# Page requests of the sample group's attention: a block's second sequence asked for by ScalarE, its first by SyncE

## The reference

```python
xn = rmsnorm(x, ln1_g)
qa, ka, va, pb, gates = jnp.split(xn @ w_in, SPLIT_IN, axis=-1)
y_a = attend(qa, ka, va).reshape(B, T, WIDTH_A) @ w_br_a          # block-sparse attention
y_b, wkv_new, shift_new = rwkv7_branch(pb, ...); y_b = y_b @ w_br_b  # a recurrence over the tokens
h = x + (g_a * y_a + g_b * y_b) @ w_o
... ConvFFN: w_up, causal convolution, SiLU gate, w_down, final rmsnorm

# attention of the sample group (moba_sample), for each of 8 sequences and 8 heads
k_full = cache_k[page_table]      # 32 pages of 128 tokens = 16 blocks of 256 tokens
gate = q . mean(k of a block);  the best 3 blocks of each query are kept
probs = softmax over the kept blocks and the 8 new tokens;  out = probs @ v
```

## Time and profile before

| what | value |
|---|---|
| median of 3 executions (range) | 1322.64 us (1315.37 to 1325.59) |
| the profiled execution: its own time, its span | 1318.78 us, 1316.7 us |
| mean granted TensorE clock | 0.976 of full speed |
| PE busy over the span | 1212.2 us, 92% |
| ACT busy over the span | 409.8 us, 31% |
| bytes moved by all transfers | 216.28 MB, of which 142.80 MB from 210 to 654 us |

### The profile page before, as it was taken

How to read it: one execution, slowest core, us unless ns; L and a number is a source line. 1 busy time by engine, 2 the same in 40 slices (tenths; PEclk the granted TensorE clock), 3 DMA queues, 4 the chain that set the end, 5 groups by cost and what they waited for, 6 DMA issues and landing times. The chain is left out here.

```text
span 1316.7 us, 33244 instructions
## 1 busy us (share of the span) xinstructions
PE 1212.2 (92%) x14362; PEld 1105.5 (84%) x14362; DVE 628.0 (48%) x1066; ACT 409.8 (31%) x765; POOL 433.4 (33%) x299
## 2 busy tenths in 40 slices
PE   6999997998889888976789999989999999999995
PEld 6988996666766667654589999989999999999994
DVE  6467896444554654555662223234555544470003
ACT  5142331333334332223522222333344333342110
POOL 2333453001110111010123334625555555563440
PEclk9999999999999999998789999999999999999998
DMA  5221215997898789798312222221222222222211
GB/s 210 97 101 72 72 51 232 389 346 292 303 386 329 276 328 380 279 368 304 128 64 82 81 81 97 82 90 65 81 84 92 82 81 81 93 89 89 89 57 72
DMA packets 57252, 216.28 MB, mean 164 GB/s; under 512 B 6610, under 2 KB 6995, under 8 KB 56339
## 3 DMA queue, kind: packets, MB, share of 16 engines
q1 hardware_dynamic: 57106, 214.17, 44.2%
HBM read 207.78 MB, written 6.37 MB: 163 GB/s over the span
## 5 line engine op out<-in xcount | busy, mean ns | idle before, releaser
L642 PE MATMUL ps<-buffer_at 128*128 128x288 f32 (+2 forms) x5760 | 778.3, 298 | 9.9 <-POOL buffer_at L1459 5.0
L642 PEld LDWEIGHTS ps<-buffer_at 128*128 128x128 f32 x5760 | 774.1, 191 | 15.1 <-issue 9.2
L1459 POOL TENSOR_TENSOR buffer_at<-buffer_at 128x1024 fp32r<-128x1024 f32 (+1 forms) x118 | 331.1, 2807 | 359.5 <-ACT buffer_at L1192 358.9
L1192 ACT ACTIVATE buffer_at<-buffer_at 128x1024 fp32r<-128x1024 f32 (+1 forms) x118 | 128.9, 1095 | 288.1 <-PE ps L642 135.0
L1511 POOL TENSOR_TENSOR buffer_at<-buffer_at 128x256 f32<-128x256 f32 x45 | 40.3, 925 | 320.7 <-DVE buffer_at L1751 320.7
L2113 DVE TENSOR_TENSOR buffer_at<-ps,buffer_at 128x512 f32<-128x512 f32 x44 | 30.4, 692 | 126.1 <-PE ps L642 126.1
L1430 ACT ACTIVATE buffer_at<-buffer_at 128x592 f32<-128x592 f32 x44 | 38.8, 882 | 162.4 <-DVE buffer_at L2115 159.2
L1027 PE MATMUL ps<-buffer_at 128*32 128x128 f32 x2048 | 73.5, 282 | 8.4 <-issue 5.2
L1851 DVE TENSOR_REDUCE buffer_at<-ps 128x1 f32<-128x256 f32 (+1 forms) x68 | 28.0, 411 | 109.1 <-PE ps L994 108.9
L994 PE MATMUL ps<-buffer_at 128*32 128x256 f32 x1024 | 69.6, 384 | 5.5 <-DMA buffer_at<-in_kvcache 4.2
L1027 PEld LDWEIGHTS ps<-buffer_at 128*32 128x32 f32 x2048 | 54.4, 112 | 19.3 <-issue 11.5
(11 more groups left out here) (230 smaller groups left out, 1293.9 us busy)
## 6 DMA issues: line engine op xcount, KB each, us to landing
buffer_at<-in_kvcache SPq DMA_DIRECT2D x256, 512.0 KB, 6.1
buffer_at<-in_w_up SPq DMA_DIRECT2D x44, 512.0 KB, 3.5
buffer_at<-in_w_in SPq DMA_DIRECT2D x42, 512.0 KB, 3.5
buffer_at<-in_w_down SPq DMA_DIRECT2D x16, 704.0 KB, 4.1
buffer_at<-in_w_br SPq DMA_DIRECT2D x8, 512.0 KB, 3.5
buffer_at<-in_w_o SPq DMA_DIRECT2D x8, 512.0 KB, 3.5
buffer_at<-in_xin SPq DMA_DIRECT2D x4, 576.0 KB, 7.1
buffer_at<-in_xin SPq DMA_DIRECT2D x1, 2304.0 KB, 11.1
```

The costliest lines, as they stand in the source:

```text
L642: ins = e.matmul(out, lhs, rhs[:, cols], start=(start and i == 0), stop=(stop and i == 2))
L1192: e.activation(hi[:, :, :], raw, ACT.Copy).then_inc(w_hi, 1)
L1459: e.tensor_tensor(lo[:, :, :], raw, hi[:, :, :], ALU.subtract).then_inc(w_lo, 1)
```

## The change

A helper pages_of loads the two page numbers of one sequence into registers of the engine named, and a helper pages_in requests its two pages on that engine. The first three fills stay with SP whole. For each later fill (61 of them) SP loads and requests only the pair's first sequence, after the same wait as before. The second sequence is ACT's: in step i it loads the page numbers of fill step_fill(i) + 3 behind pt_out(i), and requests the two pages behind o_out(i), that is behind the wait for the pv_step whose slot they go into. Each slot still counts four landings.

```diff
+        def pages_of(f, s, engine):
+            at = (2 * (f // NBLK) + s) * NPG + 2 * (f % NBLK)
+            return nc.values_load_multi_w_load_instructions(ptab[0:1, at:at + 2], engines=(engine,), min_val=0,
+                                                            max_val=kvcache.shape[0] - 1)[1]
+
+        def pages_in(e, f, s, found):
+            for a, pg in enumerate(found):
+                e.dma_start(kvring[slot_of(f)][:, 2 * s + a, :],
+                            kvcache[bass.ds(pg, 1)].rearrange("o p n -> p (o n)")).then_inc(kv_fill[slot_of(f)], 16)
...
             def fill(f):
-                p, j = f // NBLK, f % NBLK
-                found = [nc.values_load_multi_w_load_instructions(
-                    ptab[0:1, (2 * p + s) * NPG + 2 * j:(2 * p + s) * NPG + 2 * j + 2], engines=(mybir.EngineType.SP,),
-                    min_val=0, max_val=kvcache.shape[0] - 1)[1] for s in range(2)]
+                mine = range(2) if f < RING else range(1)
+                found = [pages_of(f, s, mybir.EngineType.SP) for s in mine]
                 if f >= RING:
                     e.wait_ge(sa_pv, fill_step(f - RING) + 1)
-                for s in range(2):
-                    for a, pg in enumerate(found[s]):
-                        e.dma_start(kvring[slot_of(f)][:, 2 * s + a, :],
-                                    kvcache[bass.ds(pg, 1)].rearrange("o p n -> p (o n)")).then_inc(kv_fill[slot_of(f)], 16)
+                for s in mine:
+                    pages_in(e, f, s, found[s])
...
             for i in range(STEPS):
                 pt_out(i)
+                nxt = step_fill(i) + RING if i % PER else FILLS
+                if nxt < FILLS:
+                    found = pages_of(nxt, 1, mybir.EngineType.Activation)
                 attention(UNIT_AT.get((i - 1, 3)))
                 chunk_copies(CHUNK_AT.get((i, 0)))
                 end_work(i, 0)
                 chunk_copies(CHUNK_AT.get((i, 1)))
                 attention(UNIT_AT.get((i, 1)))
                 o_out(i)
+                if nxt < FILLS:
+                    pages_in(e, nxt, 1, found)
                 if i + 1 < STEPS:
                     exp_step(i + 1)
```

## The result

The changed kernel takes 1332.22 us in the median (6 runs, 1329.52 to 1338.61), the kernel before beside it 1319.51 us (6 runs, 1315.37 to 1325.59). The ratio is 1.0087, 95% interval 1.0059 to 1.0115: 12.7 us slower by the medians, under the 1% that counts as a change here, and close to the 1330 us forecast. Run again beside other kernels it was 1.0106 times the time before (1.0065 to 1.0147), a little over that 1%. It is a small loss, and both intervals lie above 1.

A forecast was written before the change was run, and what follows sets the result against it. In the loop PE was taken to wait mostly for ACT's exponentials, not transfers. −2 + 5 + 1.5 + 3 + 1.5 = +9 us gave 1328 by the profile, 1332 by the median; forecast 1330 us, range 1318 to 1354.

The forecast's parts named there:

- the requests fit, the late steps pay: The forecast case: ACT's requests fit before the exponentials except where ACT comes late; 1322 to 1336 us, chance 0.58.
- The price of a pair: Two page requests on ACT, between result copy and exponentials, cost 1.03 us as on SP, inside 1.26 us of cover.
- usual steps: 28 of the loop's 61 steps, with 1.26 to 1.32 us from result copy to exponentials, enough to cover ACT's requests.
- ACT pays more than its cover: Rival: between copy and exponentials ACT's requests outlast 1.26 us; over 1% slower from about 1.4 us, 1340 to 1350; chance 0.34.
- The load behind the first copy: ACT's page-number load delays work right behind its first copy in four steps, 0.77 us each; half taken, +1.5 us.
- The 12 late steps: Steps with less than 1.03 us between ACT's copy and exponentials; they lose what the requests lack in cover, +5 us.
- Slow requests: Requests over 0.4 us, partly moved from SP to ACT, delay the exponentials PE waits for: +3 us.
- Two engines asking at once: SP and ACT request after the same pv_step; if requests cannot overlap, exponentials start late: 0 to +3, taken +1.5 us.
- SP's relief: In the loop, SP's third and fourth pages are asked for 1.03 us earlier, shortening PE's page waits: −2 us.
- The signs to look for: In the loop: PE's exponential wait grows 5 to 10 us, page waits fall to about 2; 662 us afterwards unchanged.

The follow-up runs named there:

- load alone: The change with SP requesting all four pages again, while ACT only loads the page numbers and does nothing with them: 1319.68 us, ratio 0.9998 against the kernel before.
- half kernel before: The kernel before, fetching only the first 512 of 1024 columns of each page from the fourth block on: 1297.58 us, 0.9817 of before.

## Why the prediction was right, point by point

The forecast "the requests fit, the late steps pay" came true in its number, 1330 for 1332.22, and in its first half. Its sum of +9 us came near the 12.7 and 15.8 us measured by terms of other sizes: two were put too high and a third perhaps, one was too low, and one cost was not in it at all. That they nearly cancel is luck.

- **The price of a pair, 1.03 us.** Right: in half of the steps without a held request the pair ends 0.99 to 1.04 us after the copy's start; one request is 350 ns. The usual steps are unchanged, median 1.26 us. The rival that ACT pays more than its cover stood on this price, and needed 1.4.
- **The load behind the first copy, +1.5.** Not seen: load alone gives 0.9998, though 1.5 us would still lie within its interval (0.9975 to 1.0021). I put the load's 0.81 us in line with ACT's copies on paper. In the trace after all 61 loads start while one of ACT's activations still runs, which the trace of before could not show.
- **The 12 late steps, +5.** Too large. Outside the steps with held requests the exponentials lost 2.3 to 2.6 us. One reason is in a late step of the trace after, whose second request was also held (0.99 us):

```profile
421.06 0.34 ACTq L528 DMA_DIRECT2D buffer_at<-in_kvcache  x1
...
421.57 0.99 ACTq L528 DMA_DIRECT2D buffer_at<-in_kvcache  x1
...
422.19 0.27 ACT L1302 ACTIVATE buffer_at<-ps 128x128 f32<-128x128 f32 x1
422.66 0.47 ACT L1294 ACTIVATE buffer_at<-ps,buffer_at 128x256 f32<-128x256 f32 x1 [0.20 <-issue]
```

  ACT's queue issues the requests while an earlier activation still runs, 1.1 us before the copy that stands ahead of them in the program. In 10 of the 61 steps the first request starts ahead of the copy. The prediction let them start with the copy.
- **Slow requests, +3.** That slow requests reach ACT's exponentials was right, the size was off: 6.1 and 10.1 us in the two profiles. I gave ACT its share of 28 slow requests as if they came by lot. They come when an instruction block moves, and since both engines now request in the same moment, a hold that struck SP alone now mostly strikes both.
- **Two engines asking at once, +1.5.** Not seen in the records. 93 of ACT's requests overlap one of SP's by over 200 ns with neither held, and their median is 349 ns, against 343 for the 83 that overlap none in the run with ACT's requests a step later; in the usual step above both pairs run side by side. The Trainium skill (Perfetto Trace Analysis, DMA Instruction — HWDGE) has the generator locked for one request at a time and the wait inside the recorded duration. By that rule one of two requests that start together would read up to two of them, some 0.67 us (an estimate, from 0.333); this trace does not agree, outside the holds.
- **SP's relief, −2.** The waits for pages fell by 0.6 to 1.6 us. But the term had another side that the prediction did not have: two queues of pages in each other's way and, likely, in the way of PE's instructions. With one page on ACT this costs 12 us, the whole loss; in the change itself "issue" rose by about 5 us, as much as it swings between two executions.
- **The signs to look for.** PE's wait for the exponentials was to grow by 5 to 10: its row grew by 2.8 and, in the second profile, by 7.2; all time behind ACT by 8.5. The waits for pages were to fall to about 2 (2.6 and 3.6). The 662 us behind the loop stayed.

The largest thing I missed was in the page of the kernel before all along: the row of pv_step with "issue", and the queue named instruction. I had summed the waits of PE that name an engine or a transfer, and left the others as unexplained.

```profile
q8 instruction: 113, 1.85, 0.6%
...
L1027 PE MATMUL ps<-buffer_at 128*32 128x128 f32 x2048 | 73.5, 282 | 8.4 <-issue 5.2
```

## What to carry to other kernels

Issue slots on an idle engine are only free where nothing on the path stands behind them: here 0.35 us per request fits the cover, and a request of 0.5 to 2.6 us, in a quarter of the steps, mostly doesn't. Look for the longest durations of a request and for what they coincide with before moving it to an engine that also computes; on SP the same hold lay in waiting time. And a second queue is not neutral where the DMA engines are as busy as here (0.86 over the loop): one page in it cost 12 us, and 3 to 5 with half the bytes.

## What the runs showed that I had not expected

- A request for a page can be held until a 16 KB block of instructions has moved: 30 of 32 long requests end 0.37 to 0.39 us behind such a packet, on both engines together where both ask at once. Why the second of a pair stands and the first passes is not shown.
- PE's stalls for blocks of 256 instructions cost 12 to 24 us of the loop in the profiles of before and the change, and 0 and 2.1 in those with half the bytes. The half kernel before is 21.9 us faster, of which waits for pages explain only 4.2. The Trainium skill (Runtime: NRT & Kernel Launch, Instruction fetch mechanics) says that the fetch in blocks of 256 instructions is hidden by the pace at which instructions are issued; in this loop it is not.
- The granted clock does not follow PE's idle time in sum: the profile of the change has 73 us of it and 27.7 us of the loop at the lower level, that of before 58 us and also 27.7, and the kernel with the requests behind the exponentials has 67 us and 55.1. Ahead of nearly every fall PE had been idle more than in the mean of its loop; which idle time brings a fall is left open.
